# Prompt retention moved beside the gates' matmuls, decode attention left alone (hybrid decoder layer, one core)

## The chip, the cores and the metric
The kernel runs on one core of a Trainium2 chip. Its engines are TensorE (matmuls, PE in the rows, with weight loads as PEld), VectorE (DVE), ScalarE (ACT), GpSimd (POOL) and SyncE (SP), which issues nearly all transfers. The metric is the device time of one execution in microseconds: the median of three runs of the kernel before is 3123.01 us (3119.56 to 3125.0). The time of the changed kernel is what is predicted.

## The reference, cut to what matters
One inference step of a decoder layer on a prompt of 1024 tokens and on 8 sequences of 8 new tokens (64 sample tokens, each sequence with 512 past tokens in a paged cache). All of it is fp32.

```
qa, ka, va, qr, kr, vr, gr, gate_a, gate_b = split(rms_norm(x) @ w_in)   # 1024 x 11264 (22 tiles of 512 columns)
oa  = differential attention (8 heads, two softmaxes each), causal for the prompt; for a sample over its 4 pages + own keys
# retention, 4 heads, key 256, value 512; the prompt in 8 chunks of 128 tokens:
def ret_chunk(S, q, k, v):
    o = ((q @ k.T) * decay) @ v + (q * q_dec) @ S
    return exp(C * log_gamma) * S + (k * k_dec).T @ v, o
a = rms_plain(oa) * subln_g * (1 - lam_init)
r = rms_plain(orr) * silu(gr)
m = sigmoid(gate_a + ba) * (a @ w_pa) + sigmoid(gate_b + bb) * (r @ w_pb)
h = x + m @ w_o;  h = h + (silu(g) * u) @ w_down  with g, u = rms_norm(h) @ w_gu;  y = rms_norm(h)
```

The samples' retention has one chunk for each sequence and head, starting from a state that is given (32 states of 256 x 512), and returns the new states.

## The kernel before
A precise product is made of three fp32r matmuls: weights and activations are split into a high and a low part (w_h, w_l by GpSimd, L272 and L277; xt_h, xt_l by ScalarE and VectorE), and high x high, high x low and low x high are added in a bank of PSUM. Where the operands are not split, matmuls are plain fp32; the trace shows each of these as two instructions (transposes as one).

The program has three stages; the engines meet behind the first and the second (`end_stage`).

1. `pe_project` and its partners: the norm; 10 token-major weight tiles of w_in; the attention of the prompt braided with 4 more tiles (`pe_vr_attention`, written out in full); then the gates (`pe_feature_tile` from L576): 8 weight tiles, 4 row blocks (m) each, three chunks of 384, 384 and 320 tokens, 8 k, 3 passes. These run in loops, with 6 PSUM banks in a ring. Between gate matmuls stand the pieces of the samples' retention (`pe_n_piece`): in each block m one read of a sequence's state (L1829, weights of 64 columns) and two state updates (L1840, L1880 on VectorE). ScalarE takes the sigmoid of a gate bank and, for the first 16 blocks (silu), VectorE multiplies it with the bank and frees it (L619, L725); the other blocks need one sigmoid with a bias (L631).
2. The mixers (`pe_mixers`, a loop of two passes with 16 chunks each): the prompt's retention, a chunk c at a time: transposes of q and k (L1394), products (L1401), two state updates (L1408), the inner product (L1492), the product with the state (L1498), transposes of the result (L1415). The root of the norm is a power taken by GpSimd (L1696). Four times in a chunk a piece of decode attention is put between (`beside`): page transposes (L1425), scores (L1435, L1436), weights (L1445), values (L1457, L1460), transposes (L1468). A sequence takes 4 chunks. The chunk's tiles are double- or fourfold-buffered, the pages of keys and of values have one buffer each.
3. `pe_finish`: merge, output projection, FFN, final norm. The change does not touch it.

## Time and profile before
| | |
|---|---|
| median of 3 runs | 3123.01 us |
| profiled execution | 3118.55 us, span 3116.8 us |
| granted TensorE clock, mean | 0.98 |
| TensorE busy | 2960.8 us, 95% |
| VectorE, ScalarE, GpSimd busy | 1043.3, 619.9, 924.4 us |
| chain that ended last | TensorE 80%, issue 12%, VectorE 4%, DMA 2% |
| transfers | 349.47 MB, mean 112 GB/s |

Times in the profile count from the start of the span. A matmul's busy time overlaps that of the next, so the time from start to start is the price of one; the busy column of a stretch tells how much of it TensorE was not idle. The chain is the work that ended last, followed back; its "issue" is time in which the engine waited for nothing that the profile shows.

### The profile page before, as it was taken

To read this page: it belongs to the slowest core of one execution; us is meant where nothing else is said; L and a number is where in the kernel's file an instruction comes from. 1 tells how busy PE (TensorE), PEld (TensorE's weight loads), DVE (VectorE), ACT (ScalarE), POOL (GpSimd) and SP (SyncE) were. 2 spreads that over 40 slices of the span, in tenths; PEclk is the share of its full clock that TensorE was granted. 3 is DMA by queue.
4 is the path that set the end of the run, shared out by engine and by line. 5 is a ranking of instruction groups with operands and counts; after the bars stand their busy time and mean duration, and the time that the engine had idled before them with its cause. 6 is when DMAs were issued, how large, how long until landed. Compare 5 with 4: busy or idle time off the path is not lost.

```text
span 3116.8 us, 40394 instructions
## 1 busy us (share of the span) xinstructions
PE 2960.8 (95%) x15330; PEld 2439.5 (78%) x15330; DVE 1043.3 (33%) x1853; ACT 619.9 (20%) x1339; POOL 924.4 (30%) x782
## 2 busy tenths in 40 slices
PE   6999999999989999999797997999989999999998
PEld 4788887776766778777554557999779999998886
DVE  5430476566663121110133332242341111112323
ACT  3111111554542011111232331110120000001111
POOL 5334354022012223322200000443523343342521
PEclk9999999999999999999898998999989999999999
DMA  4332322332322433343566643443311221214311
GB/s 154 112 103 74 116 75 103 115 114 84 119 77 80 147 136 130 117 137 115 188 217 208 194 154 131 147 141 111 104 50 50 74 75 56 75 62 126 98 57 58
DMA packets 241445, 349.47 MB, mean 112 GB/s; under 512 B 26418, under 2 KB 138418, under 8 KB 241202
## 3 DMA queue, kind: packets, MB, share of 16 engines
q1 hardware_dynamic: 241330, 347.94, 33.5%
q8 instruction: 72, 1.18, 0.1%
q14 instruction: 43, 0.35, 0.0%
HBM read 249.91 MB, written 106.89 MB: 114 GB/s over the span
## 4 chain that ended last, share of the span: by engine, by line
PE 80%; issue 12%; DVE 4%; DMA 2%; POOL 1%; ACT 1%; SPq 0%; POOLq 0%; DVEq 0%; ACTq 0%
PE psum L438 38%; PE psum L414 25%; PE psum L940 5%; PE psum L979 2%; PE psum L1840 2%; PE psum L1003 2%; PE psum L1829 2%; PE psum L993 1%; POOL w_l L277 1%; PE psum L964 1%; POOL w_h L272 1%; DMA edge<-a_t 0%; PE psum L983 0%; DVE xt_l L2159 0%; DVE acc L2268 0%
## 5 line engine op out<-in xcount | busy, mean ns | idle before, releaser
L272 POOL TENSOR_TENSOR w_h<-stage,ones 128x512 fp32r<-128x512 f32 x372 | 416.9, 1151 | 1793.7 <-PE psum L438 950.9
L438 PE MATMUL psum<-xt_h,w_h 128*128 128x384 f32 (+1 forms) x2400 | 542.1, 334 | 23.7 <-DVE xt_l L2159 21.6
L438 PE MATMUL psum<-xt_h,w_l 128*128 128x384 f32 (+1 forms) x2400 | 529.5, 329 | 0.0
L438 PE MATMUL psum<-xt_l,w_h 128*128 128x384 f32 (+1 forms) x2400 | 529.1, 329 | 0.0
L277 POOL TENSOR_TENSOR w_l<-stage,w_h 128x512 fp32r<-128x512 f32 x372 | 491.6, 1352 | 7.4
L438 PEld LDWEIGHTS psum<-xt_h,w_h 128*128 128x128 f32 x2400 | 404.8, 189 | 101.2 <-issue 76.7
L414 PE MATMUL psum<-w_h,xt_h 128*128 128x512 f32 x1120 | 445.4, 398 | 17.0 <-ACTq L608 7.0
L414 PE MATMUL psum<-w_h,xt_l 128*128 128x512 f32 x1120 | 443.9, 396 | 0.0
L414 PE MATMUL psum<-w_l,xt_h 128*128 128x512 f32 x1120 | 443.7, 396 | 0.0
L438 PEld LDWEIGHTS psum<-xt_h,w_l 128*128 128x128 f32 x2400 | 408.5, 189 | 0.0
L438 PEld LDWEIGHTS psum<-xt_l,w_h 128*128 128x128 f32 x2400 | 408.0, 189 | 0.0
L414 PEld LDWEIGHTS psum<-w_h,xt_h 128*128 128x128 f32 x1120 | 212.2, 189 | 67.9 <-ACTq L608 7.4
L414 PEld LDWEIGHTS psum<-w_l,xt_h 128*128 128x128 f32 x1120 | 212.3, 190 | 49.7
L414 PEld LDWEIGHTS psum<-w_h,xt_l 128*128 128x128 f32 x1120 | 212.3, 190 | 48.9
L1880 DVE SCALAR_TENSOR_TENSOR acc<-acc,psum 128x512 f32<-128x512 f32 x64 | 47.9, 748 | 345.0 <-PE psum L1840 345.0
L600 ACT COPY edge<-psum 128x512 f32<-128x512 f32 (+1 forms) x90 | 52.8, 586 | 394.5 <-PE psum L414 391.7
L1034 ACT ACTIVATE acc<-psum,neg_max 128x256 f32<-128x256 f32 (+7 forms) x128 | 95.3, 744 | 141.1 <-DVE neg_max L1118 141.1
L2218 DVE TENSOR_TENSOR edge<-psum,edge 128x384 f32<-128x384 f32 (+1 forms) x66 | 35.3, 535 | 243.9 <-ACT edge L2111 238.9
L2197 DVE TENSOR_TENSOR acc<-acc,psum 128x512 f32<-128x512 f32 (+1 forms) x72 | 49.3, 685 | 192.5 <-PE psum L414 184.6
L1696 POOL TENSOR_TENSOR r_rstd<-r_var,exponent 128x1 f32<-128x1 f32 x32 | 17.5, 548 | 321.4 <-DVE r_var L1615 321.4
L2111 ACT ACTIVATE edge<-psum 128x384 f32<-128x384 f32 (+1 forms) x66 | 26.5, 475 | 433.2 <-PE psum L438 433.2
L940 PE MATMUL psum<-w_h,xt_h 128*128 128x512 f32 x256 | 112.6, 440 | 0.0
(212 smaller groups left out, 3227.5 us busy)
## 6 DMA issues: line engine op xcount, KB each, us to landing
stage<-in_w_in_dram SPq DMA_DIRECT2D x88, 512.0 KB, 5.9
proj<-edge SPq DMA_DIRECT2D x112, 256.0 KB, 2.0
stage<-in_w_gu_dram SPq DMA_DIRECT2D x44, 512.0 KB, 4.6
out_dram<-acc SPq DMA_DIRECT2D x40, 512.0 KB, 3.9
gates<-edge SPq DMA_DIRECT2D x32, 544.0 KB, 2.8
acc<-in_state_ret_dram SPq DMA_DIRECT2D x32, 512.0 KB, 5.2
k_page<-in_cache_k_dram SPq DMA_DIRECT2D x32, 512.0 KB, 5.8
v_page<-in_cache_v_dram SPq DMA_DIRECT2D x32, 512.0 KB, 6.4
```

What stands on the lines that cost most here:

```text
L272: last = nc.gpsimd.tensor_tensor(w_h[s][:, a:b, :], src, one.unsqueeze(1).to_broadcast([128, b - a, WN]), ALU.mult)
L277: last = nc.gpsimd.tensor_tensor(w_l[s][:, a:b, :], stage[h][:, a - lo:b - lo, :], w_h[s][:, a:b, :].bitcast(F), ALU.subtract)
L414: last = nc.tensor.matmul(psum[:, bank, :], x, w[s][:, k, :], start=k == 0 and n == 0, stop=k == nk - 1 and n == len(passes) - 1)
L438: ins = nc.tensor.matmul(psum[:, g(3 * j + c)[1], 0:width], w[s][:, k, m * 128:(m + 1) * 128], x[:, k, a:a + width], start=k == 0 and n == ...
L600: nc.scalar.copy(slot, psum[0:rows(t), g % RING, :]).then_inc(raw_ready, 1)
L940: last = nc.tensor.matmul(psum[:, VB + u % 2, :], x, wt[s][:, k, :], start=k == 0 and n == 0, stop=k == KD - 1 and n == len(passes) - 1)
L979: nc.tensor.matmul(psum[:, SB_ + 2 * c + a // 512, 0:width], q[r, qb % 4 * 128:(qb % 4 + 1) * 128], k_t[(2 * h + a // 512) % 3][r, 0:width ...
L1003: last = nc.tensor.matmul(psum[:, TB, 0:DV], mix_t[:, b * 128:(b + 1) * 128], v_in[(2 * h + b // 4) % 3][:, b % 4, :], start=b == 0, stop= ...
L1034: nc.scalar.activation(prob[:, c, 0:width], psum[:, SB_ + 2 * c:SB_ + 2 * c + 2, :].rearrange("p b n -> p (b n)")[:, 0:width], ACT.Exp, bi ...
L1829: last = nc.tensor.matmul(psum[0:TS, 7, :], q_own[:, b, m * TS:(m + 1) * TS], n_state[m % 4][:, b, :], start=first and b == 0, stop=m == D ...
L1840: nc.tensor.matmul(psum[:, 6, :], nk_dec[m % 2][:, b * 128:(b + 1) * 128], nv_in, start=True, stop=True).then_inc(nu_full, 1)
L2197: nc.vector.tensor_tensor(h, h, psum[0:rows(t), g % RING, :], ALU.add).then_inc(bank_free, 1)
```

## The change
The prompt's retention leaves the mixers' stage and is put between the gates' matmuls, beside the samples' retention that stands there already. The mixers' stage becomes `pe_decode`: decode attention alone.

- Gates (`pe_gates`, `act_gates`, `dve_gates`, `sp_gates`, all written out, no loop): the work is counted in groups of three matmuls (one k of one chunk), 24 x 32 = 768 of them. The gates have two banks in turn, and go through one chunk of tokens after the other instead of three side by side. A chunk of retention takes a beat of 21 groups, with five places for its pieces; 96 groups stand before the first beat.
- For the first 16 blocks ScalarE makes two instructions a bank, sigmoid and copy to SBUF, and frees it; VectorE multiplies in SBUF. For the others nothing changes.
- The samples' reads of the states are made for four sequences at a time, with weights of 16 columns, each in its own 32 output rows.
- The tiles of a chunk (qk_t, p_t, k_dec, state, r_rows, r_gate, q and k in) have one buffer, v in two; some lie in `gain`, `edge` and `rope_diff`. The root is made by VectorE in ten small instructions (`dve_root`) in place of GpSimd's power. For the samples' norm too.
- Decode (`pe_decode` and partners, written out): pages of keys and of values have two buffers each, transposed pages two banks, scores two pairs of banks; the weights, values and transposes of a sequence stand behind heads 2, 4 and 6 of the next.

The pieces of the diff are, in order: the gates' call and what replaces it; constants; the samples' reads in `pe_gates`; its beat (gate(n) is n groups of three gate matmuls); the freeing of a bank in `act_gates` and the product in `dve_gates`; VectorE's beat; the order of `pe_decode`; that of `dve_decode`.

```diff
-        with pe.Fori(0, N_FM // 2) as i:
-            for j in range(2):
-                pe_feature_tile(pe, xt_h1, xt_l1, j, i * 4 + (2 * (W_FM + j) + 1),
-                                lambda c: (i * 24 + (G_FM + 12 * j + c), (G_FM + 12 * j + c) % RING),
-                                beside=lambda m, k: pe_n_piece(pe, i, 4 * j + m, k))
-            pe_n_end(pe, i)
+        pe_gates(pe)
...
+    BT, BO, BU, BR, BG, BN, BA = 0, 1, 2, 3, 4, 6, 7
+    LAG, BEAT = 4 * 24, 21
+    UPDATES = {(1, 10): (0, 0), (1, 15): (0, 1), (1, 20): (1, 0), (2, 1): (1, 1),
+               (2, 6): (2, 0), (2, 11): (2, 1), (2, 16): (3, 0), (2, 21): (3, 1)}
...
+            if (r, x) == (1, 6):
...
+                for b in range(KT):
+                    for j in range(4):
+                        last = nc.tensor.matmul(psum[32 * j:32 * j + 16, BA, :], q_own[:, b, g % 2 * 4 + j, :],
+                                                n_state[j][:, b, :], start=False, stop=m == 5 and b == KT - 1)
...
+        for c in range(CHB):
+            update(c, 0)
+            inner(c)
+            gate(3)
+            if c:
+                rows_out(c - 1)
+            if c % NC:
+                across(c)
+            gate(4)
+            update(c, 1)
+            gate(3)
+            if c + 1 < CHB:
+                transposes(c + 1)
+            gate(4)
+            if c + 1 < CHB:
+                products(c + 1)
+            gate(7)
...
+            if row < 16:
...
+                nc.scalar.activation(edge[:, SG0 + 384 * (q % 2):SG0 + 384 * (q % 2) + width],
+                                     psum[:, BG + q % 2, 0:width], ACT.Sigmoid)
+                nc.scalar.copy(edge[:, row % 2 * T + a:row % 2 * T + a + width],
+                               psum[:, BG + q % 2, 0:width]).then_inc(sg_ready, 1)
+                act.wait_ge(sg_ready, q + 1)
+                act.sem_inc(bank_free, 1)
...
+            nc.vector.tensor_tensor(raw, raw, edge[:, SG0 + 384 * (q % 2):SG0 + 384 * (q % 2) + width],
+                                    ALU.mult).then_inc(gate_mul, 1)
...
+        for c in range(CHB):
+            at = chunk_kg(c)
+            beside.to(at + 4)
+            if c:
+                gated(c - 1)
+            new_state(c, 0)
+            beside.to(at + 7)
+            normalise(c)
+            beside.to(at + 9)
+            new_state(c, 1)
+            beside.to(at + 16)
+            if c + 1 < CHB:
+                between(c + 1)
...
+        for s in range(DB + 1):
+            for h in range(DH + 1):
+                if s < DB and h < DH:
+                    page(s, h)
+                if s < DB and h:
+                    scores(s, h - 1)
+                if s and h == 2:
+                    weights(s - 1)
+                if s and h == 4:
+                    outputs(s - 1)
+                if s and h == 6:
+                    outputs_t(s - 1)
...
+        for s in range(DB):
+            maximum(s)
+            if s + 1 < DB:
+                widen(s + 1)
+            combination(s)
+            outputs(s)
```

TensorE in the gates' stage before, from the second update of a block on (L438 are gate matmuls, L1840 the update of a sample's state; x_h and w_h are high parts):

```order
L1838 REGISTER_ALU
L1840 MATMUL psum<-acc 128x512
L438 MATMUL psum<-xt_h,w_h 128x384 x2
L438 MATMUL psum<-xt_h,w_h 128x320
L438 MATMUL psum<-xt_l,w_h 128x384 x2
L438 MATMUL psum<-xt_l,w_h 128x320
```

And now, at the first two places of a beat (L1429 are gate matmuls, L1460 an update of the prompt's state, L1466 its inner product, L1480 the transposes of the result, L1473 the product with the state, L1391 and L1396 the samples' inner product and reads):

```order
L1460 MATMUL psum<-acc,edge 128x512
L1466 MATMUL psum<-acc,gain 128x512
L1429 MATMUL psum<-xt_h,w_h 128x384
L1429 MATMUL psum<-xt_l,w_h 128x384
L1429 MATMUL psum<-xt_h,w_l 128x384
...
L1480 MATMUL psum<-ident,acc 128x128 x4
L1473 MATMUL psum<-acc 128x512 x2
L1391 MATMUL psum<-acc,gain 128x512
L1396 MATMUL psum<-acc,xs_flat 16x512 x8
```

Retention's fp32 matmuls stand where only gate matmuls and the samples' pieces stood, the three chunks of tokens of one weight block are no longer side by side, and the register instruction before a piece is gone.

VectorE in the mixers before, from a state update to the gate product (L1606 state, L1615 variance, L1596 decay of the products, L1620 normalisation, L1627 gate product; the root between L1615 and L1620 is GpSimd's):

```order
L1606 SCALAR_TENSOR_TENSOR state<-state,decay,psum 128x512
L1615 TENSOR_SCALAR r_var<-r_sq 128x1
L1595 REGISTER_ALU
L1596 TENSOR_TENSOR p_t<-psum,decay 128x128
L1620 TENSOR_SCALAR r_rows<-psum,decay,r_rstd 128x512
L1627 TENSOR_TENSOR r_gate<-psum,r_gate 128x512
```

And now, in the gates' stage (L1706 state, L1719 variance, L1604 to L1613 the root, L1722 normalisation):

```order
L1706 SCALAR_TENSOR_TENSOR acc<-acc,rope_diff,psum 128x512
L1719 TENSOR_SCALAR o_var<-o_square_sum 128x1
L1604 TENSOR_SCALAR o_seed<-o_var 128x1
L1606 TENSOR_SCALAR o_rstd<-o_seed 128x1
L1609 SCALAR_TENSOR_TENSOR o_newton<-o_rstd,o_var 128x1
L1611 SCALAR_TENSOR_TENSOR o_rstd<-o_newton,o_rstd 128x1
...
L1613 TENSOR_SCALAR o_rstd<-o_rstd 128x1
L1722 TENSOR_SCALAR acc<-psum,rope_diff,o_rstd 128x512
L1706 SCALAR_TENSOR_TENSOR acc<-acc,rope_diff,psum 128x512
```

The root now stands in VectorE's own line between the two state updates of a chunk, and the second update waits behind it.

## Rows read from the trace of the kernel before

**Rows 1.** Busy us (instructions) of PE, PEld, DVE, ACT, POOL; clock; DMA share, GB/s.
```profile
967.00:1511.00 544.00, 540.39 (x2619) 418.46 (x2617) 87.70 (x155) 77.47 (x157) 143.16 (x128) 1.00 0.38 129
1511.00:1529.00 18.00, 3.33 (x21) 2.77 (x22) 2.40 (x5) 4.76 (x8) 17.58 (x16) 0.54 0.64 190
1529.00:1691.00 162.00, 155.16 (x800) 90.08 (x800) 55.99 (x123) 53.45 (x116) 8.47 (x16) 0.99 0.67 221
1691.00:1706.00 15.00, 2.96 (x12) 2.06 (x12) 2.29 (x5) 0.67 (x2) 0.30 (x1) 0.58 0.76 241
1706.00:1869.00 163.00, 154.35 (x796) 89.73 (x796) 57.15 (x125) 53.96 (x116) 8.76 (x16) 0.99 0.53 170
1869.00:1900.00 31.00, 9.42 (x35) 7.35 (x36) 12.04 (x13) 6.43 (x7) 0.00 (x0) 0.64 0.66 236
```

**Rows 2.** Timeline (start us, us, engine, line, operation) of PE in the gates' stage.
```profile
1056.42 1.93 PE L1829 MATMUL psum<-acc 128*64 128x512 f32 x4
...
1061.46 1.12 PE L1840 MATMUL psum<-acc 64*128 64x512 f32 x2
1062.51 0.76 PE L438 MATMUL psum<-xt_h,w_h 128*128 128x384 f32 x3
...
1067.34 0.66 PE L438 MATMUL psum<-xt_l,w_h 128*128 128x384 f32 x3
...
1072.31 0.67 PE L438 MATMUL psum<-xt_h,w_l 128*128 128x384 f32 x3
1072.90 1.93 PE L1829 MATMUL psum<-acc 128*64 128x512 f32 x4
```

**Rows 3.** Timeline of PE in the mixers' stage, one chunk.
```profile
1571.10 0.60 PE L1415 MATMUL psum<-ident,r_rows 128*128 128x128 f32 x4
1571.54 1.02 PE L1408 MATMUL psum<-rv_in,k_dec 128*128 128x512 f32 x2
...
1573.83 1.88 PE L1498 MATMUL psum<-state,qk_t 128*128 128x512 f32 x4
1575.55 1.02 PE L1435 MATMUL psum<-page_t,q_wide 128*128 128x512 f32 x2
...
1577.02 1.02 PE L1408 MATMUL psum<-rv_in,k_dec 128*128 128x512 f32 x2
```

**Rows 4.** Timeline of PE in the mixers' stage, weights and values of a sequence.
```profile
1561.09 1.26 PE L1445 MATMUL psum<-s_comb,s_prob 128*128 128x64 f32 x10
...
1564.20 1.92 PE L1457 MATMUL psum<-v_page,s_mix_t 128*16 128x256 f32 x32
...
1566.60 1.98 PE L1498 MATMUL psum<-state,qk_t 128*128 128x512 f32 x4
```

**Rows 5.** Timeline of PE at the end of the prompt's attention.
```profile
959.64 2.05 PE L1003 MATMUL psum<-acc 128*128 128x128 f32 x16 [0.17 <-ACT acc L1080]
961.45 0.48 PE L940 MATMUL psum<-w_h,xs_hl 128*128 128x512 f32 x1
961.76 0.39 PE L940 MATMUL psum<-w_l,xs_hl 128*128 128x512 f32 x1
962.00 0.39 PE L940 MATMUL psum<-w_h,xs_hl 128*128 128x512 f32 x1
```

**Rows 6.** Groups by line: busy us, mean ns of one, idle before.
```profile
L619 ACT ACTIVATE edge<-psum 128x384 f32<-128x384 f32 (+1 forms) x48 | 19.2, 474 | 176.4 <-PE psum L438 176.4
...
L1553 ACT ACTIVATE s_prob<-psum,s_neg_max 128x576 f32<-128x576 f32 x8 | 5.9, 741 | 26.7 <-DVE s_neg_max L1643 26.7
```

**Rows 7.** As rows 1, four us in which many transfers are under way.
```profile
1535.00:1539.00 4.00, 3.86 (x18) 2.38 (x19) 0.84 (x2) 1.93 (x5) 0.27 (x1) 1.00 1.04 410
```

**Rows 8.** Timeline of DVE, the norm of the prompt's attention.
```profile
962.48 0.17 DVE L1152 TENSOR_SCALAR o_var<-o_square_sum 128x4 f32<-128x4 f32 x1 [5.11 <-ACT edge L1066]
...
964.66 0.16 DVE L1163 SCALAR_TENSOR_TENSOR o_rstd<-o_newton,o_rstd 128x4 f32<-128x4 f32 x1
```

**Rows 9.** One line: ns min/median/max of one, first and last start.
```profile
L684 DVE TENSOR_TENSOR edge<-edge x36: 691/693/1677, 348.4 to 537.8; 128x512 f32<-128x512 f32 x32, 64x512 f32<-64x512 f32 x4
```

More of the change, by code:

```diff
@@ L1215, in hybrid_layer @@
-    p_t = [sb(f"p_t{s}", [128, 128], F, st) for s in range(2)]
-    k_dec = [sb(f"k_dec{s}", [128, RK], F, st) for s in range(2)]
-    state = [sb(f"state{s}", [128, KT, RV], F, st) for s in range(2)]
-    r_rows = [sb(f"r_rows{s}", [128, RV], F, st) for s in range(2)]
-    r_square = sb("r_square", [128, RV], F, st)
-    r_gate = [sb(f"r_gate{s}", [128, VT, 128], F, st) for s in range(4)]
-    r_sq = [sb(f"r_sq{s}", [128, 1], F, st) for s in range(2)]
-    r_var = sb("r_var", [128, 1], F, st)
@@ new lines, in hybrid_layer @@
+    n_state = [fm_view(128, KT, RV) for _ in range(4)]
+    state = fm_view(128, KT, RV)
+    r_rows = fm_view(128, RV)
+    qk_t = fm_view(128, 2 * KT, 128)
+    rv_in = [fm_view(128, RV) for _ in range(2)]
+    rq_in, rk_in = fm_view(128, RK), fm_view(128, RK)
+    nv_in = fm_view(TS, RV)
+    nr_rows = fm_view(128, RV)
+    nq_in, nk_in = fm_view(TS, RK), fm_view(TS, RK)
+    r_gate = gain[:, 0:512].rearrange("p (b n) -> p b n", b=VT)
+    nr_gate = gain[:, 512:768].rearrange("p (b n) -> p b n", b=VT)
@@ new lines, in hybrid_layer @@
+    p_t = gain[:, 768:896]
+    np_t = gain[0:TS, 896:1024]
+    n_qdec = gain[:, 1024:1088]
+    rope_flat = rope_diff[:, :, :, :].rearrange("p t s d -> p (t s d)")
+    decay = [rope_flat[:, 132 * s:132 * (s + 1)] for s in range(2)]
+    st = ExitStack()
+    for half in ("high", "low"):
+        sb(f"under_{half}", [128, KD * T], F, st)
+    xs_flat = sb("xs_flat", [128, KD * 128], F, st)
+    st.close()
+    nqk_t = xs_flat[:, 0:256].rearrange("p (k n) -> p k n", n=TS)
+    q_own = xs_flat[:, 256:512].rearrange("p (k b r) -> p k b r", k=KT, r=16)
@@ L1372, in sp_mixers @@
+        for s in range(DB):
+            numbers = [sp.value_load(pages[0:1, s * NPG + p:s * NPG + p + 1], min_val=0, max_val=N_PHYS - 1)
+                       for p in range(NPG)]
+            if s >= 2:
+                sp.wait_ge(s_full, s - 1)
+            load_pages(numbers, s % 2, *keys)
+            if s >= 2:
+                sp.wait_ge(s_out_full, s - 1)
+            load_pages(numbers, s % 2, *vals)
         sp.wait_ge(s_norm, 5)
@@ new lines, in page, with scores @@
+        def page(s, h):
+            if h == 0:
+                pe.wait_ge(kp_loaded[s % 2], 64 * (s // 2 + 1))
+            pe.wait_ge(page_ready, max(DH * s + h - 1, 0))
+            for p in range(NPG):
+                last = nc.tensor.transpose(psum[:, BP + h % 2, p * 128:(p + 1) * 128],
+                                           k_page[s % 2][:, p, h * 128:(h + 1) * 128], ident[:, :])
+            last.then_inc(page_full, 1)
+        def scores(s, h):
+            if h == 0:
+                pe.wait_ge(wide_ready, s + 1)
+                pe.wait_ge(s_exp, max(s - 1, 0))
+            pe.wait_ge(page_ready, DH * s + h + 1)
+            q, banks = q_wide[:, h * 128:(h + 1) * 128], score_banks(s)
+            nc.tensor.matmul(banks[:, 0, :], q, page_t[h % 2][:, :], start=h == 0, stop=h == DH - 1)
+            last = nc.tensor.matmul(banks[:, 1, 0:TS], q, k_new_t[:, h, :], start=h == 0, stop=h == DH - 1)
+            if h == DH - 1:
+                last.then_inc(s_full, 1)
```

1195 lines of the change are left out of this document (591 added, 604 removed).

## The prediction
> **What bounds the kernel now.** I read the busy time of each engine in stretches first [rows 1], then the instructions in order of time in the two stages that the change touches [rows 2 to 4], and last the single prices that the new order needs [rows 5 to 9]. The gates' stage (967 to 1511 us) holds TensorE 540.4 of 544 us busy at the full clock, so it is TensorE's own work. The mixers' stage (1511 to 1869, prompt retention and decode attention braided) is nearly so: 155.2 of 162 us and 154.4 of 163 in the two passes of its loop, but there are three stretches in which TensorE has little: 18 us at its start (3.3 busy, clock 0.54), 15 us between the passes (3.0 busy) and 31 us behind it (9.4 busy) [rows 1]. The reader is to see that both stages are charged by TensorE's time. Work that moves from one to the other saves nothing by itself. What can be saved is the idle time around it; what can be lost is the price of braiding fp32 matmuls into the gates' fp32r matmuls, and waits on shorter buffers.
>
> **The gates' stage after the change, term by term.** The gate matmuls stay 8 tiles x 4 x 3 x 8 x 3 = 2304. Between 1067.34 and 1072.31 thirty of them start, 0.1657 us each [rows 2]: 381.8 us. They are now grouped by bank instead of by weights; as each has its own weight load before and after, I take that at nothing.
>
> Retention of the prompt: four transposes take 0.44 us (1571.10 to 1571.54), and one fp32 matmul of 512 columns is a pair of instructions, two of them in 1.72 us (1573.83 to 1575.55), so 0.86 [rows 3]. A chunk has transposes of q and k, products (taken like them) and transposes of the result, 3 x 0.44; two state updates and the inner product, 3 x 0.86; and the product with the state, 1.72, but for the first chunk of each head. That is 5.62 us, and 32 x 5.62 - 4 x 1.72 = 173 us.
>
> Retention of the samples: the 64 updates stay, 64 x 0.86 = 55 us; the inner product, 4 x 0.86 = 3.4, and the small transposes and products about 5. The 64 reads of the states, which cost 64 x 0.86 = 55 us before, become 8 groups of 8 matmuls of 16 output rows in four column groups. The attention's value product has this form with 256 columns: 40 instructions in 2.40 us (1564.20 to 1566.60) [rows 4], 0.06 each, so 0.12 at 512 columns, and 8 x 16 x 0.12 = 15.4 us. This is the change's one real saving on TensorE, 40 us.
>
> Switching: counted in the program, the row of gate matmuls is broken 225 times, before 108 times (27 a head). Its price: from one read of a state to the next, 1056.42 to 1072.90, pass 16.48 us with 72 gate matmuls (11.93) and four fp32 matmuls of 512 columns (3.44); the remaining 1.11 us is three breaks, 0.37 each [rows 2]. The attention stage before it is written out, not a loop: 16 instructions of 128 columns take 1.81 us where 16 x 0.1075 = 1.72 is their streaming time, and the first matmul behind them 0.31 us where the next takes 0.24, so 0.16 a break [rows 5]. The new gates' stage is written out too and has no register instructions at a break; half of its breaks hold sample pieces of odd shapes. I take 0.28, in the middle: 225 x 0.28 = 63 us, with the ends 36 and 83.
>
> The page TensorEngine Tiling (Array Packing) of the Trainium skill, section Key Properties, says that a change of the tiling mode drains TensorE. By this rule the prompt's pieces, which fill the whole array as the gates do, would break cheaply and only the sample's pieces would pay in full; about 150 breaks at 0.16 and 75 at 0.37 would make 52 us of the 63. The trace agrees so far that the pieces of 64 rows or 64 columns are those that cost 0.37 [rows 2].
>
> Waits: a bank of 24 gate matmuls takes 4.0 us of TensorE, and ScalarE needs one sigmoid of 0.47 us [rows 6] and a copy of like length to free it, so two banks are enough. ScalarE, 77 us busy in the stage, comes to about 155 of 700. VectorE gets the root that GpSimd made: the attention's norm shows twelve such small instructions, the first at 962.48 and the last at 964.66 [rows 8], 0.2 us a step, so 2.0 us for the ten here and about 0.8 for the normalisation, once in 22 us; the next user of its result (rows out, the next inner product) stands some 17 gate groups (8.5 us) behind. What else stands behind it on VectorE are state updates; a sample's update matmul waits for the one before, five groups (2.5 us) earlier. With the start of the stage I give 9 us for all waits, between 0 and 45.
>
> Sum: 381.8 + 173 + 55 + 3.4 + 5 + 15.4 + 63 + 9 = 706 us against 544, so +162 us.
>
> **The decode stage.** A head of a sequence costs TensorE 1.47 us (1575.55 to 1577.02: scores, new keys, transposes) [rows 3], eight 11.8; weights 1.2, values 2.40 [rows 4], two transposes 0.22: 15.6 us a sequence. Alone, it must wait at the turn of a sequence: the queries for the next are widened only after the mask addition and the maximum of the last, about 1.8 us behind its last score, and only 0.9 us of page transposes stand there. With that and small gaps I take 17.0. The upper end is what the braid pays: 162 us for four sequences [rows 1], 40.5 each, less 4 x 5.62 for the chunks leaves 18.0; the lower 15.6. Transfers: 32 + 32 page loads of 0.52 MB, 4.2 MB a sequence; at 410 GB/s, which the stage reaches when much is under way [rows 7], 10 us; at the 221 of the first pass [rows 1], 19. Keys and values are now double-buffered, so I expect them hidden.
>
> Start: 18 us as before, 2 until the pages are there and 3 for work at half clock; seven sequences at 17.0 make 119, the last 11.8, and then its own chain, uncovered: maximum, exponential (0.74, [rows 6]), combination, weights, values, transposes, about 9.5 us with ten handoffs. Behind it the norm and the next stage's loads, 30 of the 31 us of [rows 1]. Together 23 + 119 + 11.8 + 9.5 + 30 = 193 us. Before: 18 + 162 + 15 + 163 + 31 = 389. So -196 us, of which 15 are the gap between the passes and the rest moved work.
>
> **Sum:** +162 - 196 = -34 us. The profiled execution took 3118.55 us (span 3116.8), 4.5 below the median of 3123.01; I carry the difference over: 3089 us.
>
> **Rivals.** (1) VectorE, in order and with single buffers, holds TensorE in every beat. For it: p_t, k_dec, qk_t, r_rows and the chunk's state have one buffer where each had two, and VectorE waits for TensorE, ScalarE and transfers in one line. The small and the two-input instructions on SBUF are stretched when GpSimd works: the same addition of 128x512 took 691 ns at least and 1677 at most [rows 9]. Six such steps in the root, each 1 us later, would make the chain 6 us longer. Against it: GpSimd works 143 of 544 us [rows 1], at the start of a weight tile, where no sample updates stand, and 8.5 us of slack follow. Price: 2 us in each of 32 beats are 64 us, +30 in all, 3153 us, slower than before; it decides from 34/32 = 1.06 us a beat.
>
> The page SBUF - State Buffer of the Trainium skill, section Who interferes with whom, says that a VectorE instruction with two SBUF inputs contends with GpSimd's reads and the later one blocks fully. It speaks against taking the gate product and the root into SBUF operands; the trace agrees [rows 9], and by it the 48 products would delay GpSimd or VectorE by up to 48 us in all, beside TensorE's path.
>
> (2) The breaks cost 0.37 as in the loop, +20 us, and a sequence 18.0, +8: -6 us, 3117. For it: half of the breaks are the very pieces of [rows 2]. (3) Two banks are not enough: ScalarE comes late by 0.3 us at each of 96 banks, 29 us, and the time stays, 3118. For it: 48 banks need two instructions now. Against: 4.0 against about 1.2 us. (4) Breaks at 0.16 and no waits: -27 - 9 - 11, so -81 us, 3042.
>
> **Chances.** Forecast, a gain between 15 and 60 us: 0.60. Rival 2, gains of 6 to 15: 0.12. Rival 4: 0.05. Rival 3 and other ways to no change: 0.08. Rival 1: 0.15. A measurement tells 0.2%, 6 us, from no change. So faster 0.77, same 0.08, slower 0.15. The range leaves out the far parts of 4 and 1: 3055 to 3130 us; the likeliest case alone has 3063 to 3108.
>
> **What would show it.** The stage with the gates should be about 706 us long with TensorE over 98% busy, and its matmuls 0.166 us apart; the pieces in its breaks 0.86 us for each 512 columns, and the grouped reads about 1.9 us for 16 instructions. The stretch from its end to the next stage should be about 193 us, with 17 us a sequence, no second gap, and one wait of about 1 us a sequence for the widened queries. The forecast is wrong if TensorE waits for VectorE's or ScalarE's results by more than 1 us a beat, if a sequence waits for its pages, or if a break costs more than 0.4 us.

## The result and the profile after

The changed kernel takes 3044.3 us (median of 4 runs, 3042.52 to 3050.9) against 3122.91 for the kernel before beside it (4 runs): a ratio of 0.9753, interval 0.9736 to 0.977, or 78.6 us less. A second set of five runs gave 3045.38 against 3121.82. The forecast was 3089 us, with a range down to 3055: the direction was right, the gain more than twice as large as forecast and outside the range.

The profiled execution of the changed kernel took 3050.9 us (span 3049.1), the longest of its runs; that of before took 3118.55, 4 us under its median. So the two profiles differ by only 67.7 us. A second profile of the same changed kernel (3043.6 us of span, first experiment) differs by 73.2, of which the gates' stage and the decode stage (here up to the next stage's first matmul) hold 126.7 and -201.4 and the rest -0.3 and 1.8. Where the work ahead of the gates ends varies from 967.0 to 970.5 us among the kernels here whose code ahead of them is the same; differences of 3 us outside the two stages have no cause in the change.

The windows of the changed kernel, by the same view as [rows 1] (gates; start of the decode stage; its eight sequences; its end up to the next stage):

```profile
970.00:1640.00 670.00, 664.61 (x3306) 506.91 (x3307) 283.42 (x672) 143.34 (x321) 147.05 (x127) 1.00 0.49 159
...
1640.00:1658.00 18.00, 2.33 (x20) 1.93 (x18) 4.71 (x7) 1.11 (x2) 17.70 (x16) 0.57 0.77 239
1658.00:1790.00 132.00, 127.47 (x876) 82.68 (x876) 14.30 (x56) 49.62 (x100) 0.16 (x1) 0.98 0.64 237
1790.00:1830.00 40.00, 16.42 (x88) 11.70 (x87) 13.01 (x15) 9.59 (x13) 0.00 (x0) 0.66 0.42 157
```

The gates' stage runs from 970.5 to 1640.2 us, 669.7 long against 543.3 before: +126, where I forecast +162. TensorE is 99% busy in it at the full clock. The decode stage, up to the second start of the next stage's matmuls (1829.3), takes 189 us against 389: -200, where I forecast -196. The one gap between the two passes of the old loop is gone, the 18 us at the start, mostly idle, are as they were.

TensorE's waits in the gates' stage, two kinds in all (us in total, times, longest):

```profile
PE psum L1403 <- DVE acc L1645: 3.3, 6, 0.8
PE psum L1377 <- DMA acc<-proj: 2.0, 1, 2.0
```

TensorE waits 5.3 us, of which 3.3 for the update of a sample's state by VectorE. That small row matters below: of its six waits two (1.0 us) stand behind a root in VectorE's line, four (2.2 us) behind a gate product that itself waited for ScalarE.

The groups of TensorE's pieces (L1403 the samples' updates, L1460 the first and second update of a chunk, L1396 the reads in four column groups):

```profile
L1403 PE MATMUL psum<-acc,xs_flat 64*128 64x512 f32 x128 | 71.7, 640 | 3.3 <-DVE acc L1645 3.3
L1460 PE MATMUL psum<-acc,edge 128*128 128x512 f32 x128 | 65.3, 592 | 0.0
...
L1396 PE MATMUL psum<-acc,xs_flat 128*16 128x512 f32 x128 | 15.3, 595 | 0.0
```

The reads take 15.3 us, as worked out from the attention's like form (15.4). L1403 and L1460 stream the same 512 columns the same number of times, and one is busy 6.4 us more than the other: the first sign that breaks have two prices.

The breaks themselves, in the timeline of TensorE (start, us, engine, line). First a piece of 128 rows and 128 columns alone between gate matmuls:

```profile
1291.94 0.34 PE L1429 MATMUL psum<-xt_h,w_l 128*128 128x384 f32 x1
1292.12 1.02 PE L1460 MATMUL psum<-acc,edge 128*128 128x512 f32 x2
1292.58 0.71 PE L1429 MATMUL psum<-xt_h,w_h 128*128 128x320 f32 x1
1293.12 0.31 PE L1429 MATMUL psum<-xt_l,w_h 128*128 128x320 f32 x1
```

From 1291.94 to 1293.12 pass 1.18 us. Two gate matmuls are in it, 0.176 for 384 columns and 0.147 for 320, and the pair of 512 columns, 0.86: their sum is 1.18. The break is free. The start of the next gate matmul alone would mislead, it stands 0.46 us behind the pair's; the cost must be read over both sides.

Then a piece of 64 rows:

```profile
1333.37 0.34 PE L1429 MATMUL psum<-xt_h,w_l 128*128 128x384 f32 x1
1333.64 1.12 PE L1403 MATMUL psum<-acc,xs_flat 64*128 64x512 f32 x2
1334.69 0.45 PE L1429 MATMUL psum<-xt_h,w_h 128*128 128x384 f32 x1
1334.98 0.34 PE L1429 MATMUL psum<-xt_l,w_h 128*128 128x384 f32 x1
```

From 1333.37 to 1334.98 pass 1.61 us for 2 x 0.176 + 0.86 = 1.21: this break costs 0.40 us, the 0.37 of [rows 2] again. There 0.1 us go before the piece and 0.3 behind it. Fourteen of the 64 updates stand right behind another fp32 piece, one of the full array, and cost the same 0.39 us there: it is the shape that is paid, not the step from fp32r to fp32.

VectorE's root, from the first of its steps to the normalisation, and the spread of three of its lines (ns min/median/max of one; L1604 has one input, L1609 and L1611 have two in SBUF):

```profile
1197.63 0.15 DVE L1604 TENSOR_SCALAR o_seed<-o_var 128x1 int32<-128x1 int32 x1
...
1199.66 0.81 DVE L1722 TENSOR_SCALAR acc<-psum,rope_diff,o_rstd 128x512 f32<-128x512 f32 x1
```

```profile
L1604 DVE TENSOR_SCALAR o_seed<-o_var x36: 153/154/156, 1041.4 to 1631.4; 128x1 int32<-128x1 int32 x36
L1609 DVE SCALAR_TENSOR_TENSOR o_newton<-o_rstd,o_var x108: 219/220/1323, 1041.8 to 1632.6; 128x1 f32<-128x1 f32 x108
L1611 DVE SCALAR_TENSOR_TENSOR o_rstd<-o_newton,o_rstd x108: 158/159/1220, 1042.2 to 1632.9; 128x1 f32<-128x1 f32 x108
```

The root takes 2.0 us and the normalisation 0.81, as forecast, but not everywhere: in 8 of the 36 roots some steps with two inputs last up to 1.32 us, and the root takes 3.6 to 7.4 us instead of 1.9. TensorE waits behind none of these eight.

A turn of a sequence in the decode stage (L1839 transposes of pages, L1948 the widened queries, L1849 scores, L1912 the load of a function table, L1907 the copy of transposed pages):

```profile
1672.49 1.04 PE L1839 MATMUL psum<-ident,k_page 128*128 128x128 f32 x8
...
1673.73 1.28 ACT L1912 ACT_TABLE_LOAD   x1
...
1674.07 1.12 PE L1849 MATMUL psum<-page_t,q_wide 128*128 128x512 f32 x2 [0.54 <-DVE q_wide L1948]
...
1676.39 1.12 PE L1849 MATMUL psum<-page_t,q_wide 128*128 128x512 f32 x2 [0.58 <-ACT page_t L1907]
```

This turn starts at 1672.49 and the next at 1690.02, 17.5 us later; those behind it start at 1706.70, 1723.38, 1740.06, 1756.74 and 1773.42, 16.68 us each. Only the first turn has the load of the function table and with it the second wait.

### The profile page after: what moved, and what is told of

Its sections match the earlier page's. It is cut to its first block and busy times, and to the rows that moved or that the text cites. A ratio compares the mean times of both kernels' runs of the same rounds, so it can differ in the third digit from the quotient of the medians.

```text
span 3049.1 us, 39764 instructions
## 1 busy us (share of the span) xinstructions
PE 2910.7 (95%) x15330; PEld 2430.9 (80%) x15330; DVE 1139.5 (37%) x2178; ACT 626.5 (21%) x1371; POOL 912.1 (30%) x750
## 5 line engine op out<-in xcount | busy, mean ns | idle before, releaser
L413 PE MATMUL psum<-w_h,xt_h 128*128 128x512 f32 x1120 | 447.3, 399 | 17.6 <-ACTq L574 7.7
L437 PE MATMUL psum<-xt_h,w_h 128*128 128x384 f32 (+1 forms) x1632 | 361.4, 330 | 22.8 <-DVE xt_l L2255 20.7
L437 PE MATMUL psum<-xt_l,w_h 128*128 128x384 f32 (+1 forms) x1632 | 360.7, 329 | 0.0
L437 PE MATMUL psum<-xt_h,w_l 128*128 128x384 f32 (+1 forms) x1632 | 360.5, 329 | 0.0
L1429 PE MATMUL psum<-xt_h,w_h 128*128 128x384 f32 (+1 forms) x768 | 298.7, 389 | 0.0
L437 PEld LDWEIGHTS psum<-xt_h,w_h 128*128 128x128 f32 x1632 | 277.8, 189 | 24.8 <-DVE xt_l L2255 22.6
L437 PEld LDWEIGHTS psum<-xt_h,w_l 128*128 128x128 f32 x1632 | 278.3, 189 | 0.0
L437 PEld LDWEIGHTS psum<-xt_l,w_h 128*128 128x128 f32 x1632 | 277.9, 189 | 0.0
L1429 PE MATMUL psum<-xt_h,w_l 128*128 128x384 f32 (+1 forms) x768 | 252.8, 329 | 0.0
L1429 PE MATMUL psum<-xt_l,w_h 128*128 128x384 f32 (+1 forms) x768 | 252.6, 329 | 0.0
L1429 PEld LDWEIGHTS psum<-xt_h,w_h 128*128 128x128 f32 x768 | 144.9, 189 | 75.0 <-issue 74.0
L1429 PEld LDWEIGHTS psum<-xt_l,w_h 128*128 128x128 f32 x768 | 145.2, 189 | 19.1 <-issue 19.1
L1429 PEld LDWEIGHTS psum<-xt_h,w_l 128*128 128x128 f32 x768 | 144.7, 188 | 0.0
```

The source lines that it names most:

```text
L413: last = nc.tensor.matmul(psum[:, bank, :], x, w[s][:, k, :], start=k == 0 and n == 0, stop=k == nk - 1 and n == len(passes) - 1)
L437: ins = nc.tensor.matmul(psum[:, g(3 * j + c)[1], 0:width], w[s][:, k, m * 128:(m + 1) * 128], x[:, k, a:a + width], start=k == 0 and n == ...
L1429: last = nc.tensor.matmul(psum[:, BG + q % 2, 0:width], wt[s][:, k, m * 128:(m + 1) * 128], x[:, k, a:a + width], start=k == 0 and n == 0, ...
```

## The experiments

All are timed beside the kernel before, whose medians in the three sets were 3121.82, 3122.58 and 3122.33 us; differences below are to the changed kernel's 3045.38 unless another is named. The theory after the comparison of the traces: a break by a piece that fills the array is free, and only one by a piece of another shape costs 0.37 to 0.40.

**The changed kernel again.** No edit.

> The changed kernel itself, once more, as the mark for the runs beside it. Its first profiled execution took 3050.9 us, its three other runs 3042.5 to 3045.2. Theory: 3044 us again, 78 us below the kernel before, the gates' stage (last transposes of the attention to the last product with the gates) 670 us and the decode stage behind it 178 us. Rival: the 3050.9 us is the usual time, and the median comes out near 3051.

3045.38 us (3042.74 to 3046.36), ratio 0.9754 (0.974 to 0.9767). The 3050.9 of the first profile was the odd one. The gates' stage is 670.0 us long again, and from it to the next stage's first matmul pass 176.4 us, 177.8 in the first profile.

**Samples' updates over 128 rows.**

```diff
-    nv_in = fm_view(TS, RV)
+    nv_in = fm_view(128, RV)
...
-    np_t = gain[0:TS, 896:1024]
+    np_t = gain[:, 896:1024]
...
-    nk_dec = [xs_flat[0:TS, 512 + RK * s:512 + RK * (s + 1)] for s in range(2)]
+    nk_dec = [xs_flat[:, 512 + RK * s:512 + RK * (s + 1)] for s in range(2)]
...
+        for x in (nk_dec[0], nk_dec[1], nv_in):
+            dstep.done(nc.vector.memset(x[TS:128, :], 0.0))
```

> The changed kernel with the 64 state updates of the samples (and the 4 inner products) made over 128 rows instead of 64: the upper 64 rows of both operands are zeros, so the result is the same and the streamed columns too. Theory A (a piece that fills the array breaks the row of gate matmuls at no cost, a piece of 64 rows costs about 0.37 us): 64 x 0.37 = 24 us less than the changed kernel, about 3021 us, and the gates' stage 646 us. Rival B (a break costs 0.16 us whatever its shape, as I had it for written-out code): no difference, 3044 us. Rival C (the 0.37 us are the switch from fp32r to fp32 alone): no difference either.

3022.41 us (3019.93 to 3024.48), ratio 0.968 (0.9667 to 0.9694): 23.0 us less, 0.36 for each of the 64 updates (in the timelines 0.39, from 1.25 us for an update and its break to 0.86). One of them in the timeline:

```profile
1318.97 0.34 PE L1429 MATMUL psum<-xt_h,w_l 128*128 128x384 f32 x1
1319.14 1.02 PE L1403 MATMUL psum<-acc,xs_flat 128*128 128x512 f32 x2
1319.60 0.74 PE L1429 MATMUL psum<-xt_h,w_h 128*128 128x384 f32 x1
1320.18 0.34 PE L1429 MATMUL psum<-xt_l,w_h 128*128 128x384 f32 x1
```

1.21 us from the first to the last, which is the streaming time alone. The streamed columns, the places and the type are the same, and TensorE's waits for these updates nearly so (4.1 us against 3.3); only the rows are doubled. Rivals B and C fall.

**More breaks of the free kind.** The transposes and the products of a beat are each cut in two:

```diff
             for x, a in ((rq_in, 0), (rk_in, KT)):
+                if a:
+                    between()
...
             if c + 1 < CHB:
-                transposes(c + 1)
-            gate(4)
+                transposes(c + 1, lambda: gate(1))
+            else:
+                gate(1)
+            gate(3)
```

> The changed kernel with three pieces of each beat of the prompt (transposes of q and k, products, transposes of the result) cut in two, with one group of three gate matmuls between the halves: 93 more breaks, all by pieces of 128 rows and 128 columns, nothing else added. Theory A (such a break is free): the same time as the changed kernel within 3 us, 3044. Rival B (0.16 us each): +15 us, 3059. Rival D (0.37 us each, as in the kernel before): +34 us, 3078.

3047.49 us (3044.61 to 3050.11), ratio 0.9761 (0.9748 to 0.9774): 2.1 us for 93 breaks, 0.02 each, and the intervals overlap. In the trace 228 breaks are by full pieces alone, against 145; the other ten cuts fell beside a sample's piece. By 83 it is 0.03 each. Rivals B and D fall. Between the two halves of the transposes:

```profile
1301.16 0.34 PE L1429 MATMUL psum<-xt_h,w_l 128*128 128x384 f32 x1
1301.34 0.38 PE L1486 MATMUL psum<-ident,acc 128*128 128x128 f32 x2
1301.47 0.42 PE L1429 MATMUL psum<-xt_h,w_h 128*128 128x384 f32 x1
1301.73 0.34 PE L1429 MATMUL psum<-xt_l,w_h 128*128 128x384 f32 x1
```

0.57 us, of which two gate matmuls are 0.35: 0.11 for each transpose, nothing for the break.

**The same edit of the rows in the kernel before.** The loop stays, with its register and semaphore instructions at the breaks; nv_in and nk_dec become 128 rows high as above.

> The kernel before with the 64 state updates of the samples made over 128 rows, the upper 64 rows of both operands zeros; its result is the same, and the code stays a loop with the same register and semaphore instructions at each break. Theory A (the shape of the piece makes the price of a break): 64 of 108 breaks become free, 64 x 0.37 = 24 us less, 3098 us. Rival E (the price in the kernel before was that of the loop's register instructions at a break): less than 5 us, 3120.

3099.66 us (3097.15 to 3101.64), ratio 0.9924 (0.9911 to 0.9938): 22.9 us less than before. The update of [rows 2], now on 128 rows:

```profile
1061.09 0.66 PE L438 MATMUL psum<-xt_h,w_l 128*128 128x384 f32 x3
1061.59 1.02 PE L1842 MATMUL psum<-acc 128*128 128x512 f32 x2
1062.04 1.07 PE L438 MATMUL psum<-xt_h,w_h 128*128 128x384 f32 x3
1062.95 0.66 PE L438 MATMUL psum<-xt_l,w_h 128*128 128x384 f32 x3
```

1.86 us for six gate matmuls (2 x 0.499) and 0.86: free, in the loop too. Rival E falls. My difference between "in a loop, 0.37" and "written out, 0.16" was no difference of the code.

**Reads of the states not grouped.**

```diff
-                        last = nc.tensor.matmul(psum[32 * j:32 * j + 16, BA, :], q_own[:, b, g % 2 * 4 + j, :],
-                                                n_state[j][:, b, :], start=False, stop=m == 5 and b == KT - 1)
+                        last = nc.tensor.matmul(psum[:, BA, :], xs_flat[:, 256 + 128 * b:384 + 128 * b],
+                                                n_state[j][:, b, :], start=False, stop=m == 5 and b == KT - 1 and j == 3)
```

> The changed kernel with the 64 reads of the samples' states as 64 products with a whole array of weights (128 output columns) instead of 16 columns in four column groups side by side; the number of breaks stays. It leaves out the right weights, so the samples' retention is not computed. Theory (a product costs its streamed columns, four column groups stream together): 64 products of 0.86 us twice over the two row blocks, as before the change 55 us in all, against 15.4 us: +40 us, less up to 3 us as eight changes of the tile shape go: about 3082 us. Rival (the grouping hides nothing, the cost is per instruction or per byte): less than +15 us.

3083.06 us (3082.28 to 3088.83), ratio 0.9876 (0.9861 to 0.9891): 37.7 us more. The group of the reads:

```profile
L1396 PE MATMUL psum<-acc,xs_flat 128*128 128x512 f32 x128 | 56.6, 595 | 0.0
```

56.6 us of busy time against 15.3, 41.3 more; the other 3.6 are near the 3 us of eight changes of shape. The saving of 40 us that the prediction named as the change's one real saving is there.

**Gate matmuls bank by bank, in the kernel before.** The order `for c: for k: for n` in place of `for k: for n: for c`, the pieces at the same places of the row.

> The kernel before with the one part of the change that I took at nothing: the gate matmuls of a tile row go bank by bank (24 for one bank, then the next) instead of three banks for each weight tile; the samples' pieces stay in the same places of the row, the buffers too. Theory (each matmul has its own weight load in both orders): within 3 us of the kernel before, 3122. Rival (three matmuls that share their weights in a row load them faster, or hide a longer load): 5 us or more slower.

3121.85 us (11 runs, 3118.49 to 3124.09), ratio 0.9996 (0.9987 to 1.0005). The order costs nothing that can be told (2 us at most by the interval), as taken.

**A longer root.** Twenty small instructions ahead of each root:

```diff
+        for _ in range(2):
+            for _ in range(5):
+                dstep.done(nc.vector.tensor_scalar(z, v, 1.0, None, ALU.mult))
+                dstep.wait(dve)
+                dstep.done(nc.vector.tensor_scalar(y, z, 1.0, None, ALU.mult))
+                dstep.wait(dve)
```

> The changed kernel with twenty more small VectorE instructions, each waiting for the one before, ahead of the root of every chunk (and of each head of the samples): about 20 x 0.2 = 4 us later, 36 times. Theory (8.5 us of slack stand between the root and the next product that needs it, as forecast): no difference, 3045 us, and TensorE's waits in the gates' stage stay under 10 us. Rival 1 of the prediction (VectorE in order holds TensorE in every beat): 32 x 4 = 128 us more, or a large part of that.

3111.67 us (3107.28 to 3112.69), ratio 0.996 (0.9946 to 0.9973): 66.3 us more, where I expected none. Nearly the whole gain of the change is lost by 3.8 us a root on an engine that is 42% busy in the stage. TensorE's largest waits up to 1702 us, when this stage ends:

```profile
PE psum L1403 <- DVE acc L1651: 32.3, 14, 8.3
PE psum L1460 <- DVE acc L1712: 11.7, 6, 3.6
```

One such place, on VectorE and then on TensorE (L1728 normalisation, L1651 the sample's update; the chunk's second, L1712, is between them):

```profile
1198.55 0.81 DVE L1728 TENSOR_SCALAR acc<-psum,rope_diff,o_rstd 128x512 f32<-128x512 f32 x1
...
1199.93 0.74 DVE L1651 SCALAR_TENSOR_TENSOR acc<-acc,rope_diff,psum 128x512 f32<-128x512 f32 x1
```

```profile
1200.82 2.04 PE L1403 MATMUL psum<-acc,xs_flat 64*128 64x512 f32 x2 [3.52 <-DVE acc L1651]
```

TensorE does not wait for the normalisation, which has the 8.5 us of slack that I gave it, but for the sample's update that stands behind it in VectorE's order. And the wait is paid twice: the pair behind it takes 2.04 us where it else takes 1.12; from 1200 to 1203 us the granted clock is 0.50, the lower of its two levels (1.2 GHz). Over the stage it is 0.96 instead of 1.00:

```profile
970.00:1702.00 732.00, 684.16 (x3295) 517.91 (x3293) 386.83 (x1390) 143.90 (x321) 144.78 (x125) 0.96 0.45 145
```

The stage is 64 us longer than in the changed kernel; the waits grew by 42 (47.1 against 5.3), and the other 22 are near the 29 that a clock of 0.96 makes of 732 us.

**Half of it.** Ten instructions, in the same place.

> The changed kernel with ten small instructions ahead of each root, 10 x 0.19 = 1.9 us, half of those in the run before. Theory (the sample's next update matmul stands about 2.5 us behind its VectorE step, and 3.3 us of waits are there already, so the slack is nearly used up and every further microsecond is paid in those beats in which an update stands behind the root): between a quarter and a half of the 66 us, 15 to 30 us, about 3065. Rival (a slack of 8.5 us as forecast, passed by the run before only through the clock that fell): under 3 us.

3061.82 us (3061.11 to 3062.88), ratio 0.9804 (0.9791 to 0.9818): 16.4 us more. The main wait, of 16 us of waits in all:

```profile
PE psum L1403 <- DVE acc L1649: 12.5, 10, 4.5
```

So 1.9 us cost 16 and 3.8 us cost 66: where a sample's update stands behind a root, the slack is nearly used up in the changed kernel already, and beyond it the price rises faster than the delay. The eight long roots of the changed kernel end 1.7 to 5.6 us late and cost TensorE nothing: VectorE's next sample's update comes 8.2 us or more behind them.

**The twenty instructions spread over the beat.** In the 32 chunks only; the four roots of the samples get none. `dve_filler(dve, 2)` makes four of the small instructions.

```diff
             new_state(c, 1)
+            for x in range(5):
+                beside.to(at + 10 + x)
+                dve_filler(dve, 2)
             beside.to(at + 16)
```

> The changed kernel with the same twenty small VectorE instructions for each chunk as in the run that lengthened the root, but in five lots of four between the later steps of the beat, none ahead of the root. Theory (VectorE is 42% busy, what TensorE waited for is the sample's update that stood behind one long row of waited-for instructions): at most 5 us more than the changed kernel, 3050 us. Rival (VectorE's whole work in a beat is the limit): the same 66 us more as with the lengthened root.

3060.49 us (3058.54 to 3061.71), ratio 0.9798 (0.9784 to 0.9811): 15.1 us more, not 66, and not under 5. Most of the 66 came from the place, the long unbroken row ahead of a sample's update; but the work is not free elsewhere either. Other waits take its place, the largest of them of the inner product for the decayed products (L1702):

```profile
PE psum L1466 <- DVE gain L1702: 9.0, 5, 3.3
PE psum L1403 <- DVE acc L1651: 5.0, 10, 0.8
```

**ScalarE frees a bank later.** Two more copies, each waited for, ahead of the sigmoid of the first 48 banks:

```diff
+                for x in range(2):
+                    nc.scalar.copy(edge[:, SG0 + 384 * (q % 2):SG0 + 384 * (q % 2) + width],
+                                   psum[:, BG + q % 2, 0:width]).then_inc(extra, 1)
+                    act.wait_ge(extra, 2 * q + x + 1)
```

> The changed kernel with two more ScalarE copies, each waited for, ahead of the sigmoid of each of the first 48 banks: a bank is freed some 1.2 us later. Theory (a bank of 24 gate matmuls takes TensorE 4 us and ScalarE 1.2, so two banks leave over 2 us): no difference, 3045 us. Rival 3 of the prediction (two banks are just not enough): 48 x 1.2 = 58 us more, or at least 20.

3057.2 us (3054.04 to 3060.66), ratio 0.9789 (0.9776 to 0.9803): 11.8 us more, between the theory's 0 and the rival's 58. Not one gate matmul waits for its bank; the largest wait is again that for a sample's update, 9.1 us against 3.3:

```profile
PE psum L1404 <- DVE acc L1650: 9.1, 7, 1.7
```

Two banks are enough, as forecast; what I left out is that VectorE waits in its line for the later copy, and the sample's update stands behind the product. VectorE ahead of one of these waits (L1672 the gate product, L1650 the update; TensorE's matmul starts at 1016.26, having waited 1.73 us):

```profile
1014.90 0.56 DVE L1672 TENSOR_TENSOR edge<-edge 128x384 f32<-128x384 f32 x1 [5.44 <-ACT edge L1546]
1015.38 0.74 DVE L1650 SCALAR_TENSOR_TENSOR acc<-acc,rope_diff,psum 128x512 f32<-128x512 f32 x1
```

**A version with more edits.** The updates over 128 rows, and in the decode stage:

```diff
-    q_wide = sb("q_wide", [128, DH * 144], F, st)
+    q_wide = [sb(f"q_wide{s}", [128, DH * 144], F, st) for s in range(2)]
...
-                if s and h == 0:
+                if s and h == (1 if s < DB else 0):
                     exponential(s - 1)
...
         for s in range(DB):
-            maximum(s)
             if s + 1 < DB:
                 widen(s + 1)
+            maximum(s)
...
             load_pages(numbers, s % 2, *keys)
+            if s == 0:
+                sp.dma_start(comb[:, :], c_comb).then_inc(comb_loaded, 16)
+                sp.dma_start(new_mask[:, :, :], c_new_mask).then_inc(mask_loaded, 16)
```

The page table is loaded at the start of the gates' stage, into a free corner of `edge`.

> The changed kernel with four edits: updates of the samples over 128 rows (23 us less by the run before); two buffers for the widened queries, and the exponential behind the second page copy of the next sequence instead of the first (waits of 0.54 and 0.58 us at seven turns of a sequence, 8 us); and in the decode stage's start the page table loaded in the gates' stage, the first pages ahead of the mask and the combination table (first page transposes at 18 us now, 4 to 5 us earlier). Theory: 3045 - 23 - 8 - 4.5 = 3010 us. Rival (the time at half clock at the start and the later page loads take the gains of the decode stage back): 3020 us.

3022.53 us (3017.99 to 3023.4), ratio 0.9677 (0.9664 to 0.9691). The updates alone had 0.968: the decode edits bring nothing that can be told. In the profiles the decode stage from the last gate matmul to the next stage's first is 174.2 us against 177.9 with the updates alone, 4 us instead of 12.5. Two of my terms were misread. The 0.58 us for the page's copy stands at the first turn only, not at seven; and this wait of each turn is new:

```profile
PE psum L1855 <- ACT page_t L1913: 2.3, 7, 0.3
```

Of the 0.54 us so 0.33 stay. At the start the first page transposes stand 17.6 us behind the last gate matmul instead of 18.7: SyncE issues the pages' transfers 9.4 us behind it instead of 10.6, and the 8.2 us from their issue to the transposes stay (8.1 before).

**Weights, values and transposes one head later.** Besides the edits before:

```diff
-                if s and h == 2:
+                if s and h == (3 if s < DB else 2):
                     weights(s - 1)
```

and likewise 5 for 4 and 7 for 6, on ScalarE too.

> The version with the four edits (updates over 128 rows, queries widened ahead, exponential behind the second page, earlier pages), and besides the weights, values and their transposes of a sequence one head later in the next sequence. Its profile showed a turn of 16.44 us against 16.68, because the 2.9 us of waits for the combination table took the place of those removed. Theory (one head later these waits are gone, 0.4 us a sequence, and the two smaller ones): 3 to 5 us less, 3018 us, the turn at 16.0. Rival (the page loads, 4.2 MB a sequence at about 250 GB/s or 16.7 us, set the turn): no difference, 3022, and waits for pages appear.

3019.59 us (3016.87 to 3023.59), ratio 0.9671 (0.9658 to 0.9684). 2.9 us less, inside the intervals. The turns are 16.41 us, not 16.0, and TensorE waits for no page inside a sequence. The expectation read one wait wrongly: 2.5 of the 2.9 us (L1865 for L1972) are one wait, that of the last sequence, which has nothing beside it; moving a head saves 0.4. Still this has the lowest median: 102.7 us under the kernel before, some 25 under the changed one, and nearly all of that is from the 128 rows.

## Why the prediction was wrong

**The step that failed** is the term "225 x 0.28 = 63 us" for the breaks, with its lower end of 36. 80 breaks of the stage are samples' pieces of 64 rows, of 64 columns or in column groups (64 updates, 8 reads, 8 transposes and products of the inputs), and cost 0.36 to 0.40 us: about 31 us, of which the updates make 25. The other 145 fill the array and cost 0.00 to 0.03. The term should have been 31; it was 32 too high. The two prices are shown from both sides: 93 free ones added, 64 dear ones made free in this kernel and in the one before. For the 16 other dear ones no run changed the shape, their price is read from timelines. A count was off too: "half of its breaks" hold samples' pieces, says the prediction, and 80 of 225 do.

What the forecast has as a loss was a gain. By the 0.37 of [rows 2] the 108 breaks of the stage before cost 40 us, so 63 meant 23 us more; the changed stage pays 9 us less, mainly as the grouped reads break the row 8 times instead of 32.

I had the rule in hand. By the Trainium skill, "TensorEngine Tiling (Array Packing)", section Key Properties, a change of the tiling mode drains TensorE; I used it only for a sum of 52 us beside the 63, because I still put the full-array pieces at 0.16. The runs are in line with the rule, 0.36 us a change and back, and no price for the others.

Where the 0.16 came from: [rows 5] show sixteen matmuls of 128 columns behind a wait of 0.17 us for ScalarE, so TensorE was not streaming when they began. A break with a wait in front of it was taken for the price of a break. The trace of the kernel before holds the test, in the same written-out attention: eight fp32 transposes (L993) between the matmuls of a weight tile (L940, 0.232 us each), once without an idle time in front and once with:

```profile
592.33 0.39 PE L940 MATMUL psum<-w_l,xt_h 128*128 128x512 f32 x1
592.56 1.03 PE L993 MATMUL psum<-ident,acc 128*128 128x128 f32 x8
...
593.66 0.39 PE L940 MATMUL psum<-w_h,xt_l 128*128 128x512 f32 x1
```

```profile
742.36 0.39 PE L940 MATMUL psum<-w_l,xt_h 128*128 128x512 f32 x1
742.95 1.06 PE L993 MATMUL psum<-ident,acc 128*128 128x128 f32 x8 [0.20 <-issue]
...
744.08 0.39 PE L940 MATMUL psum<-w_h,xt_l 128*128 128x512 f32 x1
```

The first takes 1.33 us for 2 x 0.232 and eight transposes of 0.109, so its break is free. The second takes 1.72: the 0.20 of idle time and 0.18 more. There are 60 such pieces without idle time, of one to eight transposes; they cost 0.11 us a transpose and nothing for the break (one of them 0.07). Of four with idle time three lose 0.18 us beyond it. The line of [rows 5] (L1003) says the same: fourteen of its matmuls with four transposes, behind the matmul at 953.81 us and without idle time, take 2.01 us, 0.11 each. So the free break stood in the trace before the change; I had priced one behind a wait. The other end, 0.37, was read correctly in [rows 2], but only at pieces of 64 rows or columns, the only kind the stage had; it bounded the new pieces of 128 rows from above and said nothing of where between zero and 0.37 they lie. The lower bound belonged at zero.

**The other steps of the gates' stage.** Gate matmuls 0.1657 us each: their spacing is 0.176 and 0.147 for 384 and 320 columns, 0.166 on the mean, and the order by banks costs nothing. Retention by its 512-column pieces of 0.86: the prediction's terms without breaks and waits add up to 633.6, and 633.6 + 31 + 5.3 = 670, which is the measured 669.7. Reads 15.3 against 15.4. Waits 5.3 against 9.

In these terms the +126 us of the stage are 173 for the prompt's retention, -40 for the reads, -9 for the breaks and 2 for waits.

**The decode stage.** Forecast 193, measured 189. Up to the end of the eighth sequence 149.9 us against 153.8 in the forecast: the start 18.0 and the first sequence 14.3, then 17.5 and six of 16.68 where I had 17.0 each. The one wait in each turn for the widened queries is there, 0.54 us against the "about 1" forecast. Pages are hidden, as forecast. Of the 200 us that this part lost, 173 are the prompt's retention, which moved, and 15 the gap between the passes; for the other 12, TensorE was idle 15.5 us in the two passes of [rows 1] and is idle 4.5 us in the eight sequences now.

**The sum.** -34 forecast; -32 for the breaks, -4 for the waits, -4 for the decode stage make -74, where the second profile shows -73. The medians, 76 to 79 apart, add that the profile of before was 4 us under its median.

**The rivals.** Rival 4 (0.16 a break, no waits, a sequence of 15.6, 3042 us) came within 3 us of the time with 0.05 of the chances, but its terms did not happen: breaks cost as much as it says in sum (31 to 36 us), by another distribution, and the waits are there. Rival 2 is false: the 0.37 holds for 80 breaks, not for 225. Rival 3 is false as put, and its experiment shows the path that it lacked. Rival 1 did not happen, 0.16 us of waits a beat are far below its 1.06. Its first link did: with GpSimd at work the steps of a root stretch, and a root ends up to 5.6 us later where that rival says 6, in 8 of 36 roots. They fall where the prediction's reason against it puts them, at the start of a weight tile with no sample's update near, and cost nothing. But my other reason, the slack, was too good. The 8.5 us hold for the root's own readers (TensorE waits for none of them even with 3.8 us more), and the prediction mentions the sample's update 2.5 us behind and makes nothing of it. That is the line which limits: 1.9 us more there cost 16 us, 3.8 cost 66.

The Trainium skill, "SBUF - State Buffer", section Who interferes with whom, has a VectorE instruction with two SBUF inputs contend with a GpSimd instruction that reads SBUF. The trace agrees: of the root's 216 steps with two such inputs (L1609, L1611) 38 are stretched, each while GpSimd splits weights; its steps with one input, named among the stretched ("the small and the two-input instructions") in the prediction, never take over 0.156 us, beside GpSimd or not. The 48 gate products, for which the prediction allows up to 48 us, are stretched by 3.0 us in all.

## What to carry to other kernels

Ask of each piece that interrupts a row of matmuls whether its rows and columns fill the array: if they do, count its streaming time and nothing else; if its rows do not, fill them with zeros where the operand has room, since the rows cost no time and the change of shape costs 0.36 us each time (no run here filled columns). Compare the sum with what the stage pays for its breaks already. A price for a break is read from the last matmul before it to the second behind it, with no wait in between, and at a piece of the same shape as the new one. Look for several places of the same kind in the trace before taking a price from one. For an engine that serves in order, the slack of a step is that of the tightest reader of anything behind it in the line, not that of its own readers.

## What the runs showed of the hardware

- fp32 matmul pairs of 512 columns on the whole array between fp32r matmuls cost 0.86 us and no more; the change of type has no price (93 more changes, 2.1 us).
- A piece of 64 rows costs 0.36 us more than the same piece over 128 rows, in a loop (22.9 us for 64) as in written-out code (23.0 us for 64).
- In the written-out attention of the kernel before, 60 full-array fp32 pieces without idle time in front cost nothing for the break; three with idle time lost 0.18 us beyond it.
- Long waits of TensorE can cost more than their length: in the run with the longer root 42 us more of waits (up to 8.3 us each) came with 22 more at a granted clock of 0.96, and the pair behind a wait of 3.52 us took 2.04 instead of 1.12.
- VectorE instructions with two SBUF inputs are stretched while GpSimd splits weights (0.22 to 1.32 us for a 128x1 step), those with one are not (0.156 us at most).
